# Prompt heads of a hybrid decoder layer: values as the stationary operand, inverse sums spread by transfers and applied by GpSimd

## The reference

```python
D_MODEL, SEQ, N_HEADS, QK_DIM, V_HEAD, Q_BLOCK = 1024, 256, 16, 96, 64, 128

def one_block(args):                      # 128 queries against 256 keys
    qb, qp = args
    s = jnp.einsum('bqhd,bkhd->bhqk', qb, k).astype(jnp.float32) * scale
    s = jnp.where(k_pos[None, :] <= qp[:, None], s, -jnp.inf)
    p = jax.nn.softmax(s, axis=-1)
    return jnp.einsum('bhqk,bkhd->bqhd', p, v)
...
o = attn_fn(q, kv_lat, k_rope)
a_out = jnp.einsum('bthd,hdo->bto', o, wts['w_attn_out'])
```

## Time and profile before

| | |
|---|---|
| Median of 3 runs | 1144.75 us (1144.63 to 1146.4) |
| Span of the profiled execution | 1143.5 us (from the first to the last instruction; a device time of this one execution is not given beside it) |
| TensorE busy | 1122.7 us, 98% of the span |
| VectorE, ScalarE, GpSimd busy | 68%, 51%, 6% |
| Chain of work that ended last | TensorE 92% |
| Prompt heads on TensorE | about 360 to 391 us |
| First page sequence | from 392.9 us |

### The profile page before, as it was taken

One profiled execution on the slowest core, in us unless ns is written; L12 is line 12 of the kernel. 1 busy time (PEld: TensorE's weight loads), 2 busy tenths in 40 slices (PEclk: granted clock), 3 DMA queues, 4 the chain that ended last, 5 costly groups with the idle time before them and its releaser, 6 DMA issues.

```text
span 1143.5 us, 25908 instructions
## 1 busy us (share of the span) xinstructions
PE 1122.7 (98%) x9549; PEld 1086.8 (95%) x9549; DVE 778.4 (68%) x1325; ACT 581.7 (51%) x1153; POOL 67.8 (6%) x136
## 2 busy tenths in 40 slices
PE   5999999999999999999999999999999999999998
PEld 3899999999898899999999999999999999999998
DVE  4655553567777688888888888888757666555543
ACT  3444453346576655455545454554566545444432
POOL 2000000010000100101010110101020010000000
PEclk9999999999999999999999999999999999999999
DMA  9987578947344440021211202032257684555552
GB/s 324 314 292 269 183 254 289 348 167 222 99 142 127 133 133 2 20 65 33 52 47 36 62 22 73 13 84 71 57 150 254 227 272 131 183 183 177 177 184 71
DMA packets 165629, 169.84 MB, mean 149 GB/s; under 512 B 25780, under 2 KB 144071, under 8 KB 165525
## 3 DMA queue, kind: packets, MB, share of 16 engines
q1 hardware_dynamic: 163799, 166.83, 45.6%
q10 hardware_dynamic: 1742, 1.88, 0.5%
HBM read 167.13 MB, written 2.49 MB: 148 GB/s over the span
## 4 chain that ended last, share of the span: by engine, by line
PE 92%; DVE 2%; SPq 2%; ACT 1%; DMA 1%; issue 1%; POOL 0%; DVEq 0%; ACTq 0%
PE PS L1894 27%; PE PS L1895 27%; PE PS L1896 27%; PE PS L1971 2%; SPq L451 2%; PE PS L2367 1%; PE PS L2342 1%; PE PS L2343 1%; DMA raw<-in_w_ffn_in 1%; PE PS L2288 1%; PE PS L2099 1%; PE PS L2308 0%; PE PS L2338 0%; DVE wL L1172 0%; PE PS L2287 0%
## 5 line engine op out<-in xcount | busy, mean ns | idle before, releaser
L1172 DVE TENSOR_TENSOR wL<-raw,wH 128x1024 fp32r<-128x1024 f32 (+2 forms) x208 | 246.3, 1191 | 209.8 <-ACT wH L717 208.4
L717 ACT ACTIVATE wH<-raw 128x1024 fp32r<-128x1024 f32 (+2 forms) x208 | 213.2, 1029 | 245.6 <-PE PS L1896 224.7
L1894 PE MATMUL PS<-uH,wH 128*128 128x264 f32 x1024 | 294.2, 287 | 4.5 <-DVE uL L1233 4.0
L1895 PE MATMUL PS<-uL,wH 128*128 128x264 f32 x1024 | 291.8, 285 | 0.0
L1896 PE MATMUL PS<-uH,wL 128*128 128x264 f32 x1024 | 291.4, 285 | 0.0
L1894 PE MATMUL PS<-wqH,kTH 128*128 128x336 f32 (+2 forms) x768 | 255.7, 333 | 0.0
L1896 PE MATMUL PS<-wqH,kTL 128*128 128x336 f32 (+2 forms) x768 | 246.1, 320 | 0.0
L1895 PE MATMUL PS<-wqL,kTH 128*128 128x336 f32 (+2 forms) x768 | 245.9, 320 | 0.0
L1894 PEld LDWEIGHTS PS<-uH,wH 128*128 128x128 f32 x1024 | 193.9, 189 | 7.9 <-issue 6.4
L1895 PEld LDWEIGHTS PS<-uL,wH 128*128 128x128 f32 x1024 | 194.2, 190 | 0.0
L1896 PEld LDWEIGHTS PS<-uH,wL 128*128 128x128 f32 x1024 | 193.6, 189 | 0.0
(11 more groups left out here) (343 smaller groups left out, 1497.8 us busy)
## 6 DMA issues: line engine op xcount, KB each, us to landing
raw<-in_w_ffn_in SPq DMA_DIRECT2D x86, 512.0 KB, 3.5
adaw<-in_w_ada SPq DMA_DIRECT2D x72, 512.0 KB, 6.5
raw<-in_w_ffn_out SPq DMA_DIRECT2D x32, 512.0 KB, 3.5
raw<-in_w_in SPq DMA_DIRECT2D x32, 512.0 KB, 4.5
kv<-in_cache_kv_latent SPq DMA_DIRECT2D x128, 128.0 KB, 2.0
raw<-in_w_ffn_out SPq DMA_DIRECT2D x16, 384.0 KB, 3.0
raw<-in_w_attn_out SPq DMA_DIRECT2D x8, 512.0 KB, 4.1
raw<-in_w_conv_out SPq DMA_DIRECT2D x8, 512.0 KB, 4.7
```

The source lines that it names most:

```text
L717: f(wH[:, k, 0:width], raw[:, k, 0:width], ACT.Copy).then_inc(w_hi, 1)
L1172: v.tensor_tensor(wL[:, k, 0:width], raw[:, k, 0:width], wH[:, k, 0:width].bitcast(F32), ALU.subtract).then_inc(w_lo, 1)
L1894: mm(dst, a[0], b[0], start=start, stop=False)
L1895: mm(dst, a[0], b[1], start=False, stop=False)
```

## The change

The scores now use three banks (0, 7, 1), and VectorE adds the mask in PSUM, only to the two squares on the diagonal (L1581 becomes an addition of 256 columns in place). The maxima and the exponentials read PSUM. The values become the stationary operand: two heads of a pair write partitions 0 to 63 and 64 to 127 of one bank, by feature instead of by token, and VectorE copies them out unscaled (`oTr`). The 16 turns, the four ScalarE copies and the waits between them leave the gates. The convolution state is turned in four parts at heads 5, 7, 9 and 11, and the first page at head 13 into bank 6.

The inverse sums are made once after the last head, turned by TensorE into 32 rows (`rlT`, head and query block by position), and SyncE copies each row to 64 partitions (`rlb`), 32 transfers of 32 KB in two parts. GpSimd multiplies `oTr` with `rlb` in two instructions of 1024 elements per partition. The second part overwrites `rlb`, so its transfers wait for the first multiplication.

```diff
+STATE_HEADS = (6, 8, 10, 12)
+PAGE_HEAD = 13
...
             sp.dma_start(wuvF[:, :, :], uv).then_inc(in_wuv, 16)
+            sp.wait_ge(rlT_done, 1)
+            sp.wait_ge(pv_ps, PAIRS)
+            for part in range(2):
+                if part == 1:
+                    sp.wait_ge(o_scaled, 1)
+                for j in range(4):
+                    for m in range(2):
+                        for t in range(2):
+                            r = H * t + 2 * (4 * part + j) + m
+                            sp.dma_start(rlb[VH * m:VH * m + VH, j, P * t:P * t + P],
+                                         rlT[r:r + 1, :].unsqueeze(1).to_broadcast([1, VH, P])).then_inc(in_rl, 16)
             with sp.Fori(1, 4) as i:
...
             pool.wait_ge(st_sb, 4)
             sample_rows(0)
+            pool.wait_ge(o_sb, 4)
+            for part in range(2):
+                pool.wait_ge(in_rl, 256 * (part + 1))
+                z = oTr[:, 4 * part:4 * part + 4, :]
+                g.tensor_tensor(z, z, rlb[:, :, :], ALU.mult).then_inc(o_scaled, 1)
             for b in range(NB):
                 pool.wait_ge(kTH_done, NPG * b + 14)
...
             def mask_max(hd):
-                v.tensor_tensor(sS[:, s, :], PS[:, s, 0:384], const[:, C_MASK:C_MASK + 384], ALU.add
-                                ).then_inc(masked, 1)
+                z = PS[:, b, :].rearrange("p (a n) -> p a n", n=P)[:, 0:3:2, :]
+                v.tensor_tensor(z, z, tri, ALU.add).then_inc(masked, 1)
...
             def heads_out(g):
-                own.done(v.reciprocal(rl[:, :, hs], ls[:, :, hs]))
-                v.tensor_tensor(otok[:, :, hs, :], PS[:, 4 + g % 2, :].rearrange("p (t h d) -> p t h d", t=2, h=4),
-                                rl[:, :, hs].unsqueeze(3).to_broadcast([P, 2, 4, VH]), ALU.mult).then_inc(o_sb, 1)
+                v.tensor_copy(oTr[:, 2 * g:2 * g + 2, :].rearrange("p j n -> p (j n)"),
+                              PS[:, VALUE_BANK[g % 2], :]).then_inc(o_sb, 1)
...
+            dve.wait_ge(exp_done, H)
+            v.reciprocal(rl[:, :, :], ls[:, :, :]).then_inc(rl_done, 1)
+            dve.wait_ge(rl_ps, 1)
+            v.tensor_copy(rlT[:, :], PS[0:2 * H, 6, KL + P:KL + 2 * P]).then_inc(rlT_done, 1)
...
-            def values(hd):
-                mm(PS[:, b, c], pTs[:, hd % 2, 0:128], vtok[:, 0, vc], start=True, stop=True)
-                mm(PS[:, b, c], pTs[:, hd % 2, 128:256], vtok[:, 0, vc], start=True, stop=False)
-                mm(PS[:, b, c], pTs[:, hd % 2, 256:384], vtok[:, 1, vc], start=False, stop=True).then_inc(pv_ps, 1)
+            def values(j):
+                for m in range(2):
+                    hd = 2 * j + m
+                    mm(PS[VH * m:VH * m + VH, b, SEQ * q:SEQ * q + SEQ], vtok[:, 0, VH * hd:VH * hd + VH],
+                       pTs[:, hd % 4, 0:256], start=True, stop=False)
+                for m in range(2):
+                    hd = 2 * j + m
+                    i_ = mm(PS[VH * m:VH * m + VH, b, SEQ * q + 128:SEQ * q + SEQ], vtok[:, 1, VH * hd:VH * hd + VH],
+                            pTs[:, hd % 4, 256:384], start=False, stop=True)
...
             gate_pair(0)
             pe.wait_ge(knsq_done, PAGES + 2)
-            turn_heads(0, 4)
-            turn_heads(1, 5)
             gate_pair(1)
```

More of the change, by code:

```diff
@@ L229, in decoder_layer @@
         qr4 = sb("qr4", [P, H // 4, 4, ROPE], at=o + 13184)
-        otok = sb("otok", [P, 2, H, VH], at=o)
+        oTr = sb("oTr", [P, KT, SEQ], at=o)
         mrg = sb("mrg", [P, KT, T], at=o + 8448)
@@ L1080, in gate_columns @@
                 f(sig[:, 2 * i:2 * i + 2, :], PS[:, GATE_BANKS[i]:GATE_BANKS[i] + 2, 0:T], ACT.Sigmoid).then_inc(g_free, 1)
[L1082 to L1097, removed]
+            for i in range(3):
+                gate_columns(i)
+            act.wait_ge(o_scaled, 2)
             act.wait_ge(ysum_done, NB)
             for kt in range(KT):
-                f(oH[:, kt, 0:SEQ], oT[:, kt, 0:SEQ], ACT.Copy).then_inc(oh_done, 1)
+                f(oH[:, kt, 0:SEQ], oTr[:, kt, :], ACT.Copy).then_inc(oh_done, 1)
             gate_columns(3)
@@ L1633, in _ @@
                     mod_columns(ADA_FFN)
[L1634 to L1638, removed]
+                    dve.wait_ge(rest_sb, 5)
+                    put_q(0, 0)
+                if hd % 4 == 2 and hd >= 6:
+                    heads_out(hd // 4 - 1)
+                if hd == PAGE_HEAD + 1:
+                    page_lo(0, 0, 0, 0, True, 6)
+            dve.wait_ge(exp_done, H)
+            v.reciprocal(rl[:, :, :], ls[:, :, :]).then_inc(rl_done, 1)
+            dve.wait_ge(rl_ps, 1)
+            v.tensor_copy(rlT[:, :], PS[0:2 * H, 6, KL + P:KL + 2 * P]).then_inc(rlT_done, 1)
             heads_out(3)
@@ L1779, in _ @@
                 dve.wait_ge(oh_done, kt + 1)
[L1780 removed]
+                v.tensor_tensor(oL[:, kt, 0:SEQ], oTr[:, kt, :], oH[:, kt, 0:SEQ].bitcast(F32), ALU.subtract
                                 ).then_inc(ol2_done, 1)
@@ L2327, in denominator, with turn @@
                 mm(PS[:, 0, 448:448 + H], ones[:, :], lsum[:, s, :], start=True, stop=True).then_inc(den_ps, 1)
-            def turn(use, s, n, pg, b, first):
+            def turn(use, s, n, pg, b, first, bank=0):
                 if n % 4 == 0:
@@ L2388, in _ @@
             pe.sem_inc(pg_rel, 8)
-            scores(0)
-            scores(1)
+            for hd in range(3):
+                scores(hd)
             for hd in range(H):
-                if hd + 2 < H:
-                    scores(hd + 2)
                 if hd == 0:
@@ L2397, in _ @@
                 turn_probs(hd)
-                if hd >= 1:
-                    values(hd - 1)
-                if hd == 14:
-                    turn_state(0)
-                if hd == 15:
-                    pe.wait_ge(masked, H)
-                    turn(0, 0, 0, 0, 0, True)
-            values(H - 1)
-            turn_state(1)
+                if hd + 3 < H:
+                    scores(hd + 3)
+                if hd >= 2 and hd % 2 == 0:
+                    values(hd // 2 - 1)
+                if hd + 1 in STATE_HEADS:
+                    turn_state(STATE_HEADS.index(hd + 1))
+                if hd == PAGE_HEAD:
+                    pe.wait_ge(st_sb, 4)
+                    turn(0, 0, 0, 0, 0, True, 6)
+            turn_sums()
+            values(PAIRS - 1)
             pe.wait_ge(o_sb, 3)
-            pe.wait_ge(pT_sb, H)
             sequence(0, 0, 0, first=True)
```

145 lines of the change are left out of this document (70 added, 75 removed).

## The result

The changed kernel takes **1157.39 us** (median of 4 runs, 1156.89 to 1159.04) against 1144.7 us: ratio 1.0109, with a 95% interval of 1.0097 to 1.0122. It is 12.7 us slower. The profiled execution is the longest of the four, 1159.04 us with a span of 1157.1; the others have spans of 1155.0 to 1155.6.

The account below looks back on a forecast made before the run. TensorE, busy 98% of the span, was taken to bound the kernel. Span 1143.5 + 3.1 (later page) + 1.5 (clock) - 1.75 (gates) = 1146.3, plus 1.25 from span to median, gives 1147.5 us; range 1143.9 to 1162.

Parts of the forecast that it names:

- likeliest case: Whole kernel: halves overlap, but the spreading's serial chain delays TensorE; 1147.5 us, own range 1143.9 to 1154.7, chance 0.48.
- heads, S: Attention heads: how much earlier the first page starts on TensorE, 4.8 us with overlap, -0.8 without.
- squares done: GpSimd's `krq`, queued behind both multiplications, would end at 444.8, with VectorE waiting for it.
- TensorE's page: Second page of the second sequence would start on TensorE at 446.4 instead of 443.26, 3.1 us later.
- One copy costs SyncE an issue: SyncE's queue in the spreading: 0.39 us per copy, bounds 0.29 and 0.51, so the 16th is issued 5.9 after the first.
- The landing: Spreading: the 16th copy of a part lands 1.7 us after its issue, as small page transfers do.
- The clock: After 7.9 us idle at the page, TensorE runs some 3 us at half speed, costing 1.5 us.
- Whatever S is: Second page of the second sequence: its start is 3.1 us later regardless of how much time the heads save.
- The halves don't overlap: Rival in the heads' value matmuls: a pair takes 1.42 us, TensorE waits 2.3, total 1146.1; chance 0.07.
- Each copy reads one partition: Rival in the spreading: single-partition reads slow the copies; 1161.3 us, 1154.4 at half effect, about 1155 by port figure; chance 0.28.
- GpSimd in time: Rival at `krq`: the chain ends by 436.9, VectorE doesn't wait, the gain stays whole, 1138.2 us; chance 0.10.
- Not spread over 16 engines: Rival in the spreading: one engine moves a copy's pieces at 20 GB/s, 1.6 us each, 1187 us at least; chance 0.04.

Follow-up runs that it names:

- e4: Changed kernel with the 32 copies each reading 64 partitions of a tile of ones instead of one partition of inverse sums: 1155.37 us, ratio 1.008.
- e10: e2 with the value matmuls ordered head by head and both heads of a pair writing the lower half of the columns: 1145.48 us, ratio 0.9996.
- e1: Changed kernel without the 32 copies and GpSimd's two multiplications, so the attention's output isn't normalised: 1140.35 us, ratio 0.9955.
- e8: Changed kernel with a pair's four value matmuls ordered both of head A, then both of head B: 1157.46 us, ratio 1.0099.
- e6: Changed kernel with the copies reading 64 rows of a constant in DRAM instead of the inverse sums: 1157.12 us (one run).
- e7: Changed kernel with each copy cut in two, 64 copies to 32 partitions each, same bytes in all: 1177.44 us (one run).
- e5: Changed kernel with all 32 copies reading one group of four partitions, the first four rows of the turned sums: 1176.58 us (one run).
- e2: Changed kernel with GpSimd's squares of the first sequence ahead of the two multiplications, copies as before: 1139.95 us, ratio 0.9946.
- e11: The kernel of e2 once more, on the same chip as e10: 1139.16 us, ratio 0.9941.
- e3: Changed kernel with SyncE issuing the 32 copies ahead of the second sequence's pages instead of behind them: 1140.44 us, ratio 0.9955.

## Why the prediction was right, and where it was off

The direction and the mechanism were right, and the time lay in the range, but 9.9 us above the forecast and outside the likeliest case's own range, whose top was 1154.7. That the stated range reached 1162 was due to a rival, the copies held by one partition's reads, which e4 rules out as the cause here: so that the time lay inside is in part luck. By its steps:

| Step | Forecast | Measured |
|---|---|---|
| pair of values | 0.71 | 0.80; 1.45 without overlap (e10) |
| heads, S | 4.8 | 4.25 |
| gates | -1.75 | -1.74 (e1) |
| first copy | 424.1 | 422.91 |
| copy to copy | 0.39 | 0.64 |
| last copy's landing | 1.7 | 2.8 |
| multiplication | 2.2 | 2.40 and 2.34 |
| squares done | 444.8 | 453.54 |
| TensorE's page | 446.4 | 455.25 |
| TensorE idle | 7.9 | 17.0 |
| lost to the clock | 1.5 | 2.9 here, 1.9 in e8 |

S is measured from the first scores to the first page (359.99 to 392.92 before, 359.04 to 387.72 after).

- **The step that failed is "One copy costs SyncE an issue".** It took 0.39 from two small stores, with bounds of 0.29 and 0.51, and 0.64 lies outside them. Over 30 steps from copy to copy that is 19.0 us (9.57 and 9.4) instead of 11.7: +7.3. With e4, e6 and e7 this is shown to be the issue's price, and not that of the transfer. No row of the kernel before had a transfer of this form.
- **The landing** was taken from page loads (1.7); twice 1.1 to 1.2 more is +2.3. e4, where the median landing falls from 2.8 to 1.9, shows that 0.9 each time is the read of a single partition, which is thus a real cost, but a small one.
- **The multiplications** cost 0.3 more, and the copies started 1.2 sooner (0.95 of it because the whole kernel was earlier there). Together: 446.4 + 7.3 + 2.3 + 0.3 - 1.2 = 455.1, against 455.25.
- **The clock** took 1.4 more than forecast, because half speed lasted 6 us of work and not 3.
- **The sum** with measured terms: 1143.5 + 12.0 (455.25 less 443.26) + 2.9 - 1.7 = 1156.7, against a span of 1157.1; a wait of 0.86 for `kTL` at 672.03 isn't in it.
- **"Whatever S is"** was right as worked out: the page's start is set by SyncE, GpSimd and VectorE alone. No run shows it with a truly slower head on the changed order, since e8 didn't slow them. TensorE's 17.0 us of idle time say it: it arrived at 438 and left at 455.25.

**The rivals.** *The halves don't overlap*: they do, by a factor of 1.8 (1.45 over 0.80) where I had 2.0 (1.42 over 0.71). *Each copy reads one partition*: its last form gave about 1155 from 0.6 us a copy, near the measured time, and was still wrong for this kernel; with 64 partitions to read from (e4) the issue takes the same 597 ns. It is true one step further on (e5). A number that fits isn't a cause. *GpSimd in time* didn't happen, but its price was right: with the squares first (e2, e11) or the copies early (e3) the time is 1139 to 1140, where that rival had 1138.2. *Not spread over 16 engines*: ruled out, since 32 KB every 0.64 us are 51 GB/s, where that rival had 20.

Left open: why this form of transfer costs SyncE 0.60 where a page load costs it 0.33, whether from SBUF or DRAM. About 0.14 of it goes with standing behind another copy (0.46 to 0.60), but the two stores at 360.23 (0.34, then 0.29) show no such rise, and no experiment has tried it.

**The version to keep** is e2: the whole computation, 0.5 to 0.6% faster than before, by placing the multiplications one step later in GpSimd's program.

## What to carry to other kernels

Work that nobody needs for 400 us is free only where its engines have nothing behind it that somebody does need: before an off-path step is placed in an in-order queue, look up the next instruction there and its reader's due time. Price a run of small transfers by the issue, of the same form, and price them serially if the second half waits for the first one's consumer. Look also at who runs beside the moved work: here VectorE was held up by GpSimd's multiplications. And when an edit is to take an overlap away, see in the trace that it did before its time is read.

## What the runs showed of the hardware

- **A transfer of 128-element rows to 64 or 32 partitions costs SyncE about 0.60 us in a row of them**, whether it reads one partition, 64, or DRAM (e4, e6, e7); the first one behind a gap took 0.46.
- **Reads of one group of four partitions run at 25 to 27 GB/s** and hold back the issuing queue (e5), but only from the sixth or seventh copy of a part on; the ones ahead of it start 0.50 to 0.87 apart. With two groups in turn, 51 GB/s went through (the changed kernel).
- **Matmuls on separate halves of the columns start out of program order** beside each other (e8: a pair takes 0.81 us), 1.8 times faster than one after the other (e10: 1.45).
- **The clock's loss doesn't grow with the idle time.** After waits of 15.2 (e4), 17.0 (after), 35.5 (e5) and 36.3 us (e7) the next four pages took 14.59, 15.39, 14.94 and 14.88 us against 12.51: 2.1 to 2.9 lost each time; e8 (16.4 idle, 14.44) lost 1.9.
- **The clock can fall without idle time.** In the profiles of e2 and e10 it was 0.50 for some 3 us in the gates, though TensorE was busy throughout; ahead of it stood small matmuls (8 rows, or 32 columns). e11 has the same matmuls and kept its clock. Between e10 and e11 it cost 1.5 us.
- **GpSimd's multiplication holds up VectorE instructions that read two tiles in SBUF.** Five such instructions that started beside one ended 0.27 to 0.29 us behind its end: convolution taps took 1.32 (e2), 1.81 (e3) and 2.60 us (e10) instead of 0.48, and the scaling of `S` 2.22 (e2) and 2.59 (e11) instead of 0.42 (e1). The sum over `krq` (e2, 436.10), which reads one tile, kept its 0.68 beside the first multiplication. TensorE then waited for `kTL`, 0.87 us at most (e3).
- **GpSimd stood 5.7 us before the reduction over partitions** that followed a multiplication (e2, "issue"), with nothing to wait for in the trace. In the kernel before, no such time shows: GpSimd waited 23.6 us there for VectorE.
